# Sums of the heaviest expert's outputs put ahead of the lo part, and output banks emptied in the order in which they are wanted

## What is computed

```
def swiglu(h, w_gate, w_up, w_down):
    return (jax.nn.silu(h @ w_gate) * (h @ w_up)) @ w_down

def moe_swiglu(h, router, w_gate, w_up, w_down):
    ...
    gates = ...            # 256 x 8, two entries a row are not zero
    y = jnp.zeros_like(hf)
    for e in range(N_EXPERTS):
        y = y + gates[:, e:e + 1] * swiglu(hf, w_gate[e], w_up[e], w_down[e])
```

## Time and profile before

| | us |
|---|---|
| median of 3 runs | 1704.34 |
| lowest and highest | 1696.85, 1709.89 |
| the profiled execution, whole | 1699.09 |
| its span, first to last instruction | 1697.3 |
| PE busy in it | 1581.5 |
| DVE, ACT busy in it | 1314.7, 841.9 |
| mean granted TensorE clock | 0.959 |

### The profile page before, as it was taken

The page is one execution under the profiler, slowest core; times in us unless marked ns, Lnnn a source line. Parts: engine busy times, 40 slices in busy tenths (PEclk is TensorE's granted clock), DMA queues, the critical chain, the costliest instruction groups (busy, mean ns, idle before and its releaser), DMA issues.

```text
span 1697.3 us, 21478 instructions
## 1 busy us (share of the span) xinstructions
PE 1581.5 (93%) x8461; PEld 1320.5 (78%) x8462; DVE 1314.7 (77%) x1445; ACT 841.9 (50%) x828; POOL 0.2 (0%) x4
## 2 busy tenths in 40 slices
PE   6989899999999987798689999999999999999994
PEld 2988787888888787566577888888898788888883
DVE  6898557777777764675458798888988888978986
ACT  6422331112112253432256777677777577767773
POOL 0000000000000000000000000000000000000000
PEclk9999899999999998799789999999999999999998
DMA  9742524544456351000189999999999999989992
GB/s 353 262 171 83 165 89 135 169 156 147 149 175 240 122 190 38 1 1 20 34 304 327 333 356 346 338 362 336 362 335 339 327 338 338 379 298 335 361 336 84
DMA packets 209452, 391.80 MB, mean 231 GB/s; under 512 B 7818, under 2 KB 82220, under 8 KB 209348
## 3 DMA queue, kind: packets, MB, share of 16 engines
q1 hardware_dynamic: 207120, 389.43, 65.5%
q10 hardware_dynamic: 2228, 0.94, 0.2%
HBM read 389.30 MB, written 1.05 MB: 230 GB/s over the span
## 4 chain that ended last, share of the span: by engine, by line
PE 83%; DVE 10%; ACT 3%; issue 2%; DMA 1%; SPq 0%; DVEq 0%; ACTq 0%
PE bank L586 20%; PE bank L588 19%; PE bank L587 19%; PE bank L2299 4%; PE bank L2300 4%; DVE lo L546 3%; DVE acc L1238 3%; PE bank L2321 2%; PE bank L2165 2%; PE bank L2154 2%; PE bank L2339 2%; ACT hi L539 2%; PE bank L2340 2%; PE bank L1865 1%; PE bank L2171 1%
## 5 line engine op out<-in xcount | busy, mean ns | idle before, releaser
L546 DVE TENSOR_TENSOR lo<-raw,hi 128x2048 fp32r<-128x2048 f32 x328 | 741.7, 2278 | 158.7 <-ACT hi L539 158.1
L539 ACT ACTIVATE hi<-raw 128x2048 fp32r<-128x2048 f32 x328 | 623.0, 1909 | 339.8 <-PE bank L588 234.0
L1238 DVE SCALAR_TENSOR_TENSOR acc<-raw,cs,acc 128x512 f32<-128x512 f32 x216 | 146.5, 744 | 2.2 <-DVE acc L1238 0.4
L2299 PE MATMUL bank<-hi,xg 128*128 128x512 f32 (+1 forms) x384 | 143.9, 382 | 2.0 <-DVE X L1735 1.8
L2300 PE MATMUL bank<-lo,xg 128*128 128x512 f32 (+1 forms) x384 | 142.3, 378 | 0.0
L586 PE MATMUL bank<-Hhi,hi 128*128 128x512 f32 x352 | 139.7, 397 | 0.0
L588 PE MATMUL bank<-Hhi,lo 128*128 128x512 f32 x352 | 138.6, 394 | 0.0
L587 PE MATMUL bank<-Hlo,hi 128*128 128x512 f32 x352 | 137.6, 391 | 0.0
L586 PE MATMUL bank<-hi,xg 128*128 128x512 f32 (+1 forms) x288 | 110.6, 384 | 3.3 <-DVE X L1735 2.3
L586 PE MATMUL bank<-H3h,hi 128*128 128x256 f32 x352 | 99.8, 284 | 11.9 <-DVE lo L546 11.9
L587 PE MATMUL bank<-lo,xg 128*128 128x512 f32 (+1 forms) x288 | 109.3, 379 | 0.0
(11 more groups left out here) (374 smaller groups left out, 3069.7 us busy)
## 6 DMA issues: line engine op xcount, KB each, us to landing
raw<-in_moe_w_gate_dram SPq DMA_DIRECT2D x88, 1024.0 KB, 6.7
raw<-in_moe_w_up_dram SPq DMA_DIRECT2D x88, 1024.0 KB, 6.9
raw<-in_moe_w_down_dram SPq DMA_DIRECT2D x88, 1024.0 KB, 6.3
raw<-in_ada_w_dram SPq DMA_DIRECT2D x48, 1024.0 KB, 7.4
raw<-in_ffn_w_gate_dram SPq DMA_DIRECT2D x11, 1024.0 KB, 5.6
raw<-in_ffn_w_up_dram SPq DMA_DIRECT2D x11, 1024.0 KB, 8.0
raw<-in_ffn_w_down_dram SPq DMA_DIRECT2D x11, 1024.0 KB, 9.8
raw<-in_ab_w_in_dram SPq DMA_DIRECT2D x6, 1024.0 KB, 13.2
```

The costliest lines, as they stand in the source:

```text
L539: nc.scalar.activation(hi[pairs[stage, key][0]][:, 0:size], raw[slot][:, 0:size], ACT.Copy).then_inc(hi_ready, 1)
L546: nc.vector.tensor_tensor(lo[slot][:, 0:size], raw[slot][:, 0:size], hi[pair][:, 0:size].bitcast(F32), ALU.subtract).then_inc(lo_ready[pai ...
L1238: ins = V.scalar_tensor_tensor(out=sum_, in0=w_, scalar=c_, in1=biased[:, place_, :] if h == 0 and i < 2 else sum_, op0=ALU.mult, op1=ALU.add)
L2299: T.matmul(b[:, 0:n_], xg[:, kk, 0:P], wh[:, k, :], start=(kk == 0), stop=False, skip_group_check=True)
```

## The change

Three things on DVE's instruction stream; PE, ACT and SP keep theirs.

- All four sums of an hd slab stand ahead of `split_lo` in their step: two in the step with back(p) = hd, ahead of the lo part of slab p, and two in the next step, ahead of the lo part of slab p + 1.
- For the hd slab that stands before (6, 20), n = 7, the order of the sums is 3, 0 and then 1, 2 instead of 0, 1 and then 2, 3.
- For the sums of rank 4, taken in the steps of (5, 3) and (5, 4), the order is 1, 2 and then 0, 3. All other ranks keep 0, 1 and then 2, 3.

```
+            def heavy_turns(n):
+
+                at = next(s for (_, s), parts in HEAVY_BEFORE.items() if ("hd", n) in parts)
+                return (3, 0, 1, 2) if at == 20 else (0, 1, 2, 3)
+
+            def rank_turns(w):
+
+                return (1, 2, 0, 3) if HEAVY_BEFORE.get((w, 5), [("", 0)])[0][0] == "hd" else (0, 1, 2, 3)
+
...
                 if w == "hu":
                     heavy_product(s)
+                for later in range(2):
+                    kind, n = back(p, later)
+                    if kind == "hd":
+                        heavy_add(n, heavy_turns(n)[2 * later:2 * later + 2])
                 if p < len(MOE):
                     split_lo(dve, "moe", MOE[p])
                 if w == "hu":
                     heavy_lo(s)
-                if w == "hd":
-                    heavy_add(s, range(2))
-                if back(p, 1)[0] == "hd":
-                    heavy_add(back(p, 1)[1], range(2, 4))
...
                     if w > 1 and s in (3, 4):
-                        add_out("moe", w - 1, gate_of(w - 1), range(2 * s - 6, 2 * s - 4))
+                        add_out("moe", w - 1, gate_of(w - 1), rank_turns(w)[2 * s - 6:2 * s - 4])
```

## The result

| | before | changed |
|---|---|---|
| median, us | 1698.4 (6 runs) | 1677.59 (6 runs) |
| lowest and highest, us | 1695.81, 1709.89 | 1676.56, 1684.51 |
| profiled execution, its span, us | 1697.3 | 1680.4 |
| granted TensorE clock in it | 0.959 | 0.963 |

The ratio is 0.9888, with a 95% interval of 0.9862 to 0.9914: 19 us less, 1.1%.

The account below looks back on a forecast made before the run. PE was taken to set the time (busy 1581.5 of 1697.3 us). Waiting 10.7 plus clock 5.1 gave 15.8 us, taken off the median 1704.34 for 1688.5; 8-in-10 range 1681 to 1698.

Parts of the forecast that it names:

- ("hd", 8): PE's wait for bank 2 (output 3): second pair of sums moves earlier, then a lo part ends the wait; gain 1.3 us.
- ("hd", 0): PE's wait for bank 1, slab (1, 4), goes: 2.26 us, plus 1.7 of clock; together 4.0 us.
- ("hd", 7): PE's 3.73 us wait for bank 6, down product of rank 6, goes, plus 1.6 of clock; together 5.3 us.
- ("hd", 10): PE's 1.31 us wait for a lo part in the last down product goes, that part coming 1.32 us earlier; gain 1.3.
- ("hd", 3): PE's waits on rank 4's sums: new order gains 2.1 us, about 2.0 stays, clock 1.8; together 3.9 us.
- the edit does more: Rival: the 5.2 us between profiled execution and median are more such stops and go too, down to 1683.3; chance 0.12.
- within 1%: Outcome over the whole kernel: measured time within 1% (17 us) of the kernel before; chance 0.65.
- faster by over 1%: Outcome over the whole kernel: measured time below 1687.3 us; chance 0.33.
- the clock as a whole stays down: Rival: falls to 1.2 GHz move elsewhere instead of going, only 10.7 us of waiting gained, 1693.6; chance 0.16.
- The loads: Rival: DMA sets the pace in the experts, gains at the first two places (7.9 us) are lost, 1696.4; chance 0.10.
- DVE next in line: Rival: the next lo part ends each wait, so five places give 1.32 us each, 6.6 in all, 1697.7; chance 0.12.
- Slower: Rival: sums delay lo parts where DVE lacks idle time, up to 15.4 us, 1719.7, half 1712; chance 0.04 including no effect.

Follow-up runs that it names:

- e2_order_only: The kernel before with only the new sum orders (slab before (6, 20) and rank 4), sums still behind the lo parts: 1691.0 us, ratio 0.9959.
- e1_ahead_only: The kernel before with the hd sums ahead of the lo part but every old sum order kept: 1685.4 us, ratio 0.9921.
- b2_before_profile: The kernel before, unchanged, run and traced a second time to see the clock behind its waits: 1696.43 us (18 runs).
- e4_all_rank_sums_ahead: The changed kernel with the sums of every light rank also ahead of the lo part of their step: 1683.2 us, ratio 0.9929.
- e3_rank_sums_ahead: The changed kernel with rank 4's sums also ahead of the lo part of their step: 1682.2 us, ratio 0.99 against the kernel before.

## Why the prediction was right and wrong

**The bound and the mechanism: right.** PE sets the time, the sums go into DVE's idle time ahead of the lo part, and the waits named are the ones that went. All that it said the profile would show is there: the two waits on L1696 are one of 2.0, the 1.31 us wait of the last down product is gone and two of 0.3 stay, and a lo part ends the wait behind ("hd", 8).

**The terms,** against the first trace of before, from which they were read. ("hd", 0): 4.0 predicted, 4.0 measured. ("hd", 7): 5.3 and 5.4. ("hd", 8) and ("hd", 10): 1.3 and 1.3 each. ("hd", 3): 3.9 and 3.0. There the waiting came out as worked out (1.96 us of it is left, and e2_order_only, without a fall, starts output 3 2.05 us earlier, where 2.1 was said). The clock term was mis-sized: "take the middle, 1.8", and 0.9 was gained, the lower end, since a fall of 3.4 us stayed in all three traces. Against the second and third trace of before, which have no fall there, this place gave only 0.6. The whole: 15.8 predicted; 15.0, 13.7 and 12.6 in the traces; 14 to 15 over the runs.

**The step that failed is the last one: "I put the gain on the median: 1688.5".** The gain was measured in one execution and then hung on a median of three runs, 1704.34, that lay 7.4 us over the mean of 67 later runs of that kernel (1696.9). 1696.9 less 15.8 is 1681.1, and the mean of the changed kernel is 1682.2. Of the 10.9 us between 1688.5 and the measured 1677.6, the wrong base is 7.4; the mean of the changed kernel lies 1.1 above 1681.1, which works the other way; and 4.6 is how far the first six runs of the changed kernel, by their median, lay under the mean of all 30. That last part is chance, or a matter of the chip, and nothing in the prediction could have given it. The right base alone would not have made 1677.6 the likely result either.

The text had seen the distance, 5.2 us between the profiled execution and that median, and made of it a case in which "the edit does more". The edit did not do more: its gain in the places is at most 15.0. What the distance was in that execution no trace shows. The third trace of before, an execution of 1704.85 us, shows what it can be: 9.7 us more than the first ahead of the experts, and 2.4 less in the five places. And the range took in the bounds of each term but nothing for the spread of single executions, which for one and the same kernel go from 1689.7 to 1709.9 (before) and from 1676.3 to 1691.9 (changed). The chances lean on the same base: "within 1%" had 0.65 and "faster by over 1%" 0.33; the first series gave 1.1%, all runs together 0.8 to 0.9%.

**At ("hd", 7) the text named one of two sufficient halves.** It gave the reason as "In the new order output 3 comes first". e2_order_only bears that out, 5.4 us by the order alone; but e1_ahead_only shows 4.9 of them without it: the second pair moves from 1516.01 to right behind the lo part of 1510.28, and is done about when PE wants the bank (0.2 us of waiting is left). The move alone was worked out for ("hd", 8) and should have been for this place as well.

**The clock: near in the sum, wrong in the rule.** The prediction had 5.1 us of clock; against the first trace of before it is 4.3 (1.7 at ("hd", 0), 0.9 at ("hd", 3), 1.7 at ("hd", 7), what the places gave beyond the waiting). The text let falls follow from the length of the wait: over 2.2 us with, 1.76 without. b2_before_profile has 2.64 and 1.19 without and 1.76 with a fall. And "each of the three falls follows a wait of over 2.2 us" left a fourth out: at 872 us, ahead of ("hd", 0), the same trace has 3.4 us at 1.2 GHz behind a wait of 1.08 us. That wait is in all fourteen traces, the fall in seven. The stretch behind it in the first and in the second trace of before:

```profile
872.20:875.40 3.20, 3.20 (x9) 2.52 (x8) 0.00 (x0) 0.00 (x0) 0.00 (x0) 0.50 0.03 13
873.00:876.50 3.50, 3.50 (x17) 2.82 (x16) 0.00 (x0) 0.70 (x1) 0.00 (x0) 1.00 0.19 70
```

What held in every trace is the simpler half: where PE no longer waits, at ("hd", 0) and ("hd", 7), there was no fall behind the place in any of the kernels that took those waits away, and where the full waits of 2.26 and 3.73 us stayed, a fall came each time. The rival that the clock as a whole stays down did not come true.

The Trainium skill (TensorE: Matmul & The Clock Gate, A second HAM failure mode: psum-queue depth-cycling) says that frequent short idle times between groups of matmuls can make the clock swing. The traces agree: a wait of 1.76 us was followed by a fall in two of five, one of 1.08 us in seven of fourteen.

**The other rivals.** The loads gave nothing back: between the places the traces agree to 0.2 us, ACT waited 0.6 us for loads in the second trace of the changed kernel (880 to 1660 us) where the earlier trace rows has 0.8, and the stretch from 1321 to 1501 us of the changed kernel, in which PE is busy for 179.67 of 180 us, moved 351 GB/s in all:

```profile
1321.00:1501.00 180.00, 179.67 (x1083) 158.30 (x1082) 160.65 (x114) 132.71 (x114) 0.00 (x0) 1.00 0.98 351
```

An experiment with smaller loads was not run; that it fell rests on the traces alone. DVE next in line came true at ("hd", 8), where a lo part ends a wait of 0.5 us, as worked out. Slower: e4_all_rank_sums_ahead put late lo parts to the test on other sums. At five of six ranks PE had slabs in hand; at rank 4 the late lo part cost a wait of 1.2 us, so the mechanism of this rival is real where DVE has no idle time and PE nothing in hand.

## What to carry to other kernels

Where one engine empties banks and also feeds the engine that fills them, look at what it waits for: an emptying put into the idle time ahead of a fed item cost nothing here and came earlier by up to the item's whole length. Where there was no idle time (rank 4 in e3_rank_sums_ahead), the fed item became the next wait, of 1.2 us. A gain read from a trace belongs on the mean of many executions of the kernel, not on the median of three; and it holds against that trace, so take a second and third trace of the kernel before as well. Where the clock of one stage moves by chance, compare the traces place by place, matmul against matmul, and let the total carry an error of its own. Two halves of a change can free the same wait; work out each alone before adding them.

## What the runs showed of the hardware

- Whether TensorE's clock falls behind a wait can be a matter of the execution: the same wait of 1.76 us was followed by 3.4 us at 1.2 GHz in one trace of the kernel before and by none in two others, a wait of 1.08 us by a fall in one and by none in two, and waits of 2.6 and 1.0 to 1.2 us by 6.8 us at half clock in one and by none in two. Behind the waits of 2.26 and 3.73 us a fall came in all four traces that have them. One trace of a kernel can't price a fall.
- A fall costs less where PE would have waited anyway: in e1_ahead_only output 3 started 2.86 us behind output 2 with the clock down, as in the first trace of before with 1.00 us of waiting in between.
- In a stage in which PE is busy for about 41 of 50 us, here the attention, the same instructions ran at a granted clock of 0.83 in one execution and of 0.56 in another. The stretch at 1.2 GHz was 17 us long in one and 44 in the other. The executions of one kernel lie up to 20 us apart (before, 73 runs), and between two traces this stage alone gives up to 12.7.
- The loads reached 388 and 389 GB/s over 5 and 3 us of the experts.
